# Hybrid attention and convolution layer on one core: prompt attention, output weights and first norm moved to other places of the program

## The reference

```python
s = jnp.einsum('bqhmd,bkhmd->bhmqk', qblk, k).astype(jnp.float32) * scale
p = jax.nn.softmax(s, axis=-1)
a = p[:, :, 0] - lam * p[:, :, 1]
return jnp.einsum('bhqk,bkhe->bqhe', a.astype(v.dtype), v)
...
att = _rms(att, subln_w) * (1.0 - lam_init)
att = att.reshape(b, n, D_ATT) * jax.nn.silu(g_att)
conv = cb * _short_conv(cc * ch, conv_w, conv_b) * jax.nn.silu(g_conv)
y = jnp.concatenate([att, conv], axis=-1) @ w_out
return x + gate * y
```

## Time and profile before

| | us |
|---|---|
| median of 3 runs (lowest, highest) | 1815.07 (1813.13, 1816.41) |
| the profiled execution, own time | 1812.12 |
| its span, first to last instruction | 1810.3 |
| PE matmul busy | 1684.4 (93%) |
| DVE busy | 1044.8 (58%) |
| ACT busy | 789.7 (44%) |
| POOL busy | 753.8 (42%) |

### The profile page before, as it was taken

The page is one execution under the profiler, slowest core; times in us unless marked ns, Lnnn a source line. Parts: engine busy times, 40 slices in busy tenths (PEclk is TensorE's granted clock), DMA queues, the critical chain, the costliest instruction groups (busy, mean ns, idle before and its releaser), DMA issues.

```text
span 1810.3 us, 25375 instructions
## 1 busy us (share of the span) xinstructions
PE 1684.4 (93%) x8526; PEld 1465.4 (81%) x8526; DVE 1044.8 (58%) x1393; ACT 789.7 (44%) x1659; POOL 753.8 (42%) x807
## 2 busy tenths in 40 slices
PE   4899999989999999999589999999999999669999
PEld 1688888879989989999468888888888888558889
DVE  2552887862242322422577777777777777465653
ACT  4562333330010100100288888888888888321110
POOL 0001888860000000000188888888888888200000
PEclk7899999999999999999899999999999999779999
DMA  9962222331020120200541141114011110455441
GB/s 358 292 199 85 105 92 104 105 120 40 31 87 15 41 75 30 73 20 30 141 104 30 35 91 45 33 31 106 29 35 55 56 32 12 148 178 188 166 150 46
DMA packets 131474, 163.69 MB, mean 90 GB/s; under 512 B 10464, under 2 KB 119776, under 8 KB 130272
## 3 DMA queue, kind: packets, MB, share of 16 engines
q1 hardware_dynamic: 126288, 158.61, 27.4%
q10 hardware_dynamic: 5136, 4.46, 0.7%
HBM read 112.95 MB, written 50.07 MB: 90 GB/s over the span
## 4 chain that ended last, share of the span: by engine, by line
PE 76%; DVE 10%; DMA 4%; issue 4%; SPq 2%; ACT 2%; ACTq 1%; POOL 1%; DVEq 0%; POOLq 0%
PE ps L688 38%; PE ps L839 11%; PE ps L914 10%; PE ps L828 9%; PE ps L820 4%; DVE stt L1494 3%; DVE e L1476 2%; PE ps L752 1%; DMA wad<-in_w_ada 1%; PE ps L897 1%; DMA worw<-in_w_out 1%; DVE w L1260 1%; DMA raw<-in_w_in 1%; DVE stt L1518 1%; DMA spill_cv<-scr 1%
## 5 line engine op out<-in xcount | busy, mean ns | idle before, releaser
L688 PE MATMUL ps<-hT,w 128*128 128x448 f32 (+1 forms) x3360 | 688.1, 365 | 12.6 <-DVE w L1260 12.6
L688 PEld LDWEIGHTS ps<-hT,w 128*128 128x128 f32 x3360 | 623.1, 188 | 70.9 <-issue 27.1
L1494 DVE TENSOR_REDUCE stt<-ps 128x1 f32<-128x1024 f32 x256 | 312.6, 1221 | 133.8 <-PE ps L839 131.7
L839 PE MATMUL ps<-kb,qb 128*128 (+1 forms) x1280 | 331.9, 390 | 46.4 <-ACT e L1154 23.6
L1154 ACT ACTIVATE e<-ps,stt 128x1024 f32<-128x1024 f32 x256 | 285.5, 1115 | 139.5 <-DVE stt L1494 139.3
L839 PEld LDWEIGHTS ps<-kb,qb 128*128 128x128 f32 x1280 | 204.3, 191 | 85.5 <-issue 38.2
L828 PE MATMUL ps<-at,vb 128*128 128x256 f32 x1088 | 272.2, 380 | 0.0
L644 POOL TENSOR_TENSOR stt<-stt,lamc 128x2 f32<-128x2 f32 x64 | 12.5, 195 | 579.0 <-DVE stt L1510 579.0
L828 PEld LDWEIGHTS ps<-at,vb 128*128 128x128 f32 x1088 | 203.7, 190 | 35.9 <-issue 0.2
L650 POOL TENSOR_TENSOR e<-e,stt 128x512 f32<-128x512 f32 (+1 forms) x192 | 218.5, 1138 | 5.0
L914 PE MATMUL ps<-mix,wo 128*128 128x448 f32 (+1 forms) x960 | 204.1, 372 | 7.2 <-DVE mix L1564 7.2
(11 more groups left out here) (120 smaller groups left out, 1383.5 us busy)
## 6 DMA issues: line engine op xcount, KB each, us to landing
raw<-in_w_in SPq DMA_DIRECT2D x32, 512.0 KB, 4.0
qb<-spill_q SPq DMA_DIRECT2D x256, 64.0 KB, 2.3
scr<-in_xtok SPq DMA_DIRECT2D x8, 1024.0 KB, 8.0
wad<-in_w_ada SPq DMA_DIRECT2D x4, 2048.0 KB, 17.0
scr<-in_xT SPq DMA_DIRECT2D x8, 1024.0 KB, 6.4
kb<-spill_k SPq DMA_DIRECT2D x8, 1024.0 KB, 9.8
spill_k<-scr SPq DMA_DIRECT2D x32, 224.0 KB, 2.2
spill_q<-scr SPq DMA_DIRECT2D x32, 224.0 KB, 2.2
```

The costliest lines, as they stand in the source:

```text
L688: mm = pe.matmul(out, slot_of(l, j), rhs_of(r, j), start=(i == 0 and j == 0), stop=(i == 2 and j == DJ - 1))
L839: mm = pe.matmul(out[:, c0 - k0:c1 - k0], qb[:, t, ver, m], keys, start=(ver == 0), stop=(ver == 1))
L1494: dve.tensor_reduce(stt[:, b, 0, 3 * m + c:3 * m + c + 1], ps[:, 2 * c:2 * c + 2, :].rearrange("p c n -> p (c n)"), AX.X, ALU.max, negate= ...
```

## The change

Four things change. The tiles in SBUF are laid out anew so that they can be: `at` loses an unused half, the prompt's buffers lie where `wo` comes to lie later, `worw` and `wo` have room of their own beside the loop's tiles, the group's tiles `atr`, `csr`, `gar`, `mixc0`, `mixa0` take over key, query and exponential buffers, `csr` of four slots replaces `csq` and `crs`, and `mix` becomes `mixc` (convolution) and `mixa` (attention).

1. The prompt's attention goes into the loop's first steps: loads ahead of the values' loads, scores on PE after step 0, DVE's six operations in steps 1 and 2, `prompt_exp` after ACT's step 1, transposes after PE's step 2, product after step 3. PE's step 4 waits for `pr_a` 3, as the value products use bank 7 as well.
2. The output weights are loaded in steps 3 to 10 and split at the ends of steps 5 to 12 (`WO0 = 5`), one tile a step.
3. The drain takes in the first group: squares in ACT's step 64, `csums` and roots after it, the four convolution halves after PE's first part of step 65, two heads' `norm` before and two behind DVE's last transposed group. There DVE makes the high part itself (`mine=True`).
4. The first group's loads of convolution and gates go out right behind the loop's last q load.

```diff
             load_q(3, 0, 3 * P)
+            load_prompt()
             load_v(0, 0)
             load_v(0, 1)
 
             sp.wait_ge(stored, 32 + 32 * H * NG)
             sp.wait_ge(aux_stored, 16 * (1 + H + H * NG))
-            load_prompt()
 
             def load_wo(n):
                 wait(sp, c_wlo, n - 1)
                 sp.dma_start(worw[:, n % 2], a["w_out"][n]).then_inc(c_raw[n % 2], 16)
...
             for it in range(ITS):
                 head = it // 4
                 for t in range(4):
-                    sp.wait_ge(s_pair, 4 * (4 * it + t + 1))
-                    if it == 4 * (H - 1) and t == 0:
-                        load_wo(0)
-                        load_wo(1)
+                    n = 4 * it + t
+                    sp.wait_ge(s_pair, 4 * (n + 1))
...
                         load_q(t, (it + 1) // 4, ((it + 1) % 4) * 4 * P + t * P)
...
+                    if WO0 - 2 <= n < WO0 - 2 + DJ:
+                        load_wo(n - WO0 + 2)
+                    if n == NT - 4:
+                        load_att(0)
+
+            load_mix(0)
+            load_gates(0)
             sp.wait_ge(t_mm, 5 * NT)
-            load_gates(0)
-            sp.wait_ge(pv_mm, NT - 2)
-            load_mix(0)
-            load_wo(6)
...
-
+            load_x(0)
             sp.wait_ge(pv_mm, NT)
+            sp.wait_ge(c_wlo, DJ)
             sp.wait_ge(aux_stored, 16 * (1 + H + H * NG + 1))
             for i in range(2):
                 sp.wait_ge(att_stored[i], 16 * ITS)
...
             def prompt_scores():
                 pe.wait_ge(s_p, 16 * (6 * H + 1))
-                pe.wait_ge(exp_done, 4 * NT)
                 for m in range(2 * H):
                     for ver in range(2):
-                        mm = pe.matmul(ps[:, m // 4, (m % 4) * P:(m % 4 + 1) * P], qp[:, ver, m], kp[:, m],
+                        mm = pe.matmul(ps[:, 5 + m // 4, (m % 4) * P:(m % 4 + 1) * P], qp[:, ver, m], kp[:, m],
                                        start=(ver == 0), stop=(ver == 1))
                 mm.then_inc(pr_mm, 1)
...
+                if isinstance(n, int) and n == 0 and g == 0:
+                    pe.wait_ge(pr_v, 2)
...
                     n = 4 * it + t
+                    if n == S_PV:
+                        pe.wait_ge(pr_a, 3)
                     step(it, t, tr=n >= S_TR, tr_last=n > S_TR, pv=n >= S_PV)
+                    if n == 0:
+                        prompt_scores()
+                    if n == 2:
+                        prompt_transposes()
+                    if n == 3:
+                        prompt_product()
             with pe.Fori(2, ITS) as it:
                 for t in range(4):
                     step(it, t)
-            prompt_scores()
-            for n in range(NT, NT + S_PV):
-                step(n // 4, n % 4, sc=False, tr=n < NT + S_TR, tr_last=n <= NT + S_TR)
-                if n == NT + 2:
-                    prompt_transposes()
-                if n == NT + 3:
-                    prompt_product()
...
+                if k < H:
+                    pe.wait_ge(exp_done, 4 * NT)
+                    bank = k
+                else:
+                    bank = 6 + k % 2
+                    if k == H:
+                        pe.wait_ge(t_dve, NT)
+                    elif k == H + 1:
+                        pe.wait_ge(att_evac, NT // 2)
+                    else:
+                        pe.wait_ge(c_std, k - 1)
+                pe.matmul(ps[:, bank, 0:n], ones, csr[:, k % 4, 0:n], start=True, stop=True).then_inc(c_sum, 1)
...
                         pe.wait_ge(c_wlo, o + 1)
                     if o == 0:
                         pe.wait_ge(c_mix[tg % 2], 32 * (tg // 2 + 1))
-                    wait(pe, o_used, k - 3)
+                    if k < H:
+                        pe.wait_ge(c_std, k + 1)
+                    else:
+                        pe.wait_ge(o_used, k - 3)
...
+            step(ITS, 0, sc=False)
             for h in range(H):
                 csums(h, GROUPS[0][1])
-                out_half(0, h, 0)
+            step(ITS, 1, sc=False, tr=False)
+            for o in range(H):
+                out_half(0, o, 0)
+            step(ITS, 1, sc=False, tr_last=False, pv=False)
+            step(ITS, 2, sc=False, tr=False)
+            step(ITS, 3, sc=False, tr=False, tr_last=False)
...
+                    if after and p == 0:
+                        for h in range(H):
+                            square(0, h)
                 if sc:
...
-                    wo_hi(0)
-                    wo_hi(1)
-                    prompt_exp()
-                if n == NT + 2:
-                    act.wait_ge(a_ready, NT)
-                    act.wait_ge(a1_ready, NT)
-                    wo_hi(2)
-                    wo_hi(3)
-                if n == NT + 3:
-                    prompt_hi()
-                    act.wait_ge(t_mm, 5 * (NT - 1))
-                    for o in range(4, DJ):
-                        wo_hi(o)
-            prompt_out()
...
-                wait(act, c_sum, k - 1)
-                act.activation(csq[:, k % 2, 0:n], atr[:, h, 0:n], ACT.Square).then_inc(c_sq, 1)
+                    act.wait_ge(c_at, 16 * (tg + 1))
+                wait(act, c_y1, k - 3)
+                act.activation(csr[:, k % 4, 0:n], atr[:, h, 0:n], ACT.Square).then_inc(c_sq, 1)
 
             def root(tg, h):
                 n = GROUPS[tg][1]
                 k = H * tg + h
                 act.wait_ge(c_sum, k + 1)
-                wait(act, c_y1, k - 1)
-                act.activation(crs[:, k % 2, 0:n], ps[:, 6 + k % 2, 0:n], ACT.Sqrt, scale=1.0 / P, bias=eps[:])\
+                bank = k if tg == 0 else 6 + k % 2
+                act.activation(csr[:, k % 4, 0:n], ps[:, bank, 0:n], ACT.Sqrt, scale=1.0 / P, bias=eps[:])\
                     .then_inc(c_std, 1)
...
+            for it in range(4):
+                for t in range(4):
+                    n = 4 * it + t
+                    step(it, t, tr=n >= S_TR, tr_last=n > S_TR, out=n >= S_OUT and t % 2 == 0, scale=n >= 1)
+                    if n == 1:
+                        prompt_exp()
+                    if n == 3:
+                        prompt_hi()
+                        prompt_out()
+                    if n == 4:
+                        act.wait_ge(aux_stored, 16 * (1 + H + H * NG + 1))
+                    if WO0 <= n < WO0 + DJ:
+                        wo_hi(n - WO0)
+            with act.Fori(4, ITS) as it:
+                for t in range(4):
+                    step(it, t, out=t % 2 == 0)
+            step(ITS, 0, sc=False, after=True)
+            for h in range(H):
+                root(0, h)
+            step(ITS, 1, sc=False, out=False, scale=False)
+            step(ITS, 2, sc=False, tr=False, scale=False)
+            step(ITS + 1, 0, sc=False, tr=False, tr_last=False, scale=False)
...
+            PROMPT_AT = {(1, 0): prompt_max, (1, 1): prompt_shift, (1, 3): prompt_den,
+                         (2, 0): prompt_coef, (2, 1): prompt_scale, (2, 2): prompt_add}
...
+                    if isinstance(n, int) and (n, p) in PROMPT_AT:
+                        PROMPT_AT[n, p]()
...
                 dve.scalar_tensor_tensor(y, atr[:, h, 0:n], sublns[:], rs, ALU.mult, ALU.mult).then_inc(c_y1, 1)
-                if h > 0:
+                if h > 0 and not mine:
                     mix_lo(tg, h - 1)
+                if h == 0:
+                    dve.wait_ge(c_ga, 16 * (tg + 1))
                 dve.wait_ge(c_y1, k + 1)
                 dve.tensor_tensor(y, y, gar[:, h, 0:n], ALU.mult).then_inc(c_y2, 1)
+                if mine:
+                    dve.wait_ge(c_y2, k + 1)
+                    dve.tensor_copy(mixa[tg % 2][:, 0, h, 0:n], y).then_inc(c_hi, 1)
+                    mix_lo(tg, h)
...
+            for it in range(4):
+                for t in range(4):
+                    n = 4 * it + t
+                    step(it, t, den=n >= 1, comb=n >= S_COMB, tr_last=n > S_TR)
+                    if WO0 <= n < WO0 + DJ:
+                        wo_lo(n - WO0)
+            with dve.Fori(4, ITS) as it:
+                for t in range(4):
+                    step(it, t)
+            step(ITS, 0, sc=False)
+            step(ITS, 1, sc=False, den=False, comb=False)
+            dve.wait_ge(a1_ready, NT)
+            dve.wait_ge(t_mm, 5 * (NT - 2))
+            norm(0, 0, mine=True)
+            norm(0, 1, mine=True)
+            step(ITS, 2, sc=False, den=False, comb=False)
+            norm(0, 2, mine=True)
+            norm(0, 3, mine=True)
```

187 lines of the change are left out of this document (80 added, 107 removed).

## The result

The change made the kernel slower: 1838.11 us, the median of 4 runs (1835.23 to 1843.58), against 1815.74 for the kernel before, timed beside it (4 runs, 1813.13 to 1820.05). The ratio is 1.0126, with a 95% interval of 1.0106 to 1.0145. The prediction had the sign right and its range holds the result, but the size not: +11.5 us forecast, +22.4 between the medians, +25.9 between the two profiled spans (1836.2 and 1810.3).

A forecast was written before the change was run, and what follows sets the result against it. PE was taken to bound the loop, busy for 580 of 599 us. The terms +28.5 + 19 - 36 = +11.5 on the profiled 1812.1 gave 1823.6, and 3.0 more for the median 1826.5 us; range 1807 to 1841.

The forecast's parts named there:

- the sign: Whole kernel: the change makes it slower, by +11.5 us on the profiled execution; chance of slower 0.71.
- Part 1: Prompt at the loop's start: PE waits for the last prompt load, then added work in the rounds; +28.5 us, ends 24 and 32.
- nothing covers the wait: Loop's start: step 1 begins 19.7 us later, uncovered because all four engines wait on PE's list.
- Part 2: Weights split in steps 5 to 12: DVE's list becomes the limit; +19 us, ends 0 and 31.
- 12.5 a step against 10.2: Weight steps: 7.9 of DVE work, 0.7 of waits inside, 3.9 at the end; first costs 2.2, seven more 2.4.
- DVE's wait for ACT: Weight steps' end: DVE's subtraction waits for ACT's exponential and factors, 1.6 us, and copy, 1.06 us.
- Part 3: Drain: attention halves begin at 1577.4 instead of 1613.40, on the earlier clock; -36 us, ends 29 and 40.
- the poorer drain: Rival, drain: convolution halves or norms meet a late load, so the gain is only 22 us; 1840.5 us, chance 0.11.
- Free weights: Rival, weight steps: DVE's subtraction slips into its waits, costing 0 instead of 19; 1807.5 us, chance 0.15.
- Contention of DVE and POOL: Rival, weight steps: POOL's work stretches DVE's subtraction by 0.87 us a step, 7 us in all; 1833.5 us, chance 0.12.
- an end of part 1: Loop's start: upper end of 32 us, if the waits hide nothing and the clock stays low for a step.

The follow-up runs named there:

- p_step1: Changed kernel with the prompt's score products one step later, behind step 1's scores, and its DVE operations moved later to match; span 1826.1 us.
- p_load: Changed kernel with the prompt's 25 loads issued ahead of the convolution's last store instead of behind it; span 1828.4 us.
- the companion: Changed kernel with PE's steps 8 to 15 written out instead of run by its loop, nothing else; span 1834.7 us, eight weight steps 107.5 us.
- w_max: Changed kernel with DVE's half of the weight split moved behind the next step's first maximum, ahead of the transposes' copy; span 1819.0 us.
- w_late: Changed kernel with DVE's half of the weight split moved from its step's end to behind the next step's second maximum; span 1814.2 us.
- w_hi_early: Changed kernel with ACT's half of the weight split moved forward, behind its copy of the step's third transposes; DVE's half stays; span 1816.8 us.
- filled3: The companion with second score products done four times in even steps 6 to 12 and twice in odd ones, filling PE's stand; span 1833.3 us.

## Why the prediction was right and wrong

**Part 1, right (+28.5; 30.5 measured).** The time of the products followed from SP's queue and the landing time within 0.2 us, once the loop's later start is taken off (892.72 less 891.04 is 1.68, not 1.64, which changes nothing). The first maximum of step 2 came at 929.93, forecast 929.2 + 1.4. The 2 us beyond the forecast are in the rounds behind it, 1.2 of them in the last, where the product was put in at 0.9 (as four matmuls; the trace has eight, 1.05 us in the drain) and took 2.08 at the low clock behind a stand of 4.4. What the prediction took as given, that nothing covers the wait, was only true of the place: p_step1 and p_load each take a third of part 1 away.

**Part 2, wrong in size (+19; 28.5 measured, 25.7 in the companion).** This is the step that failed: "12.5 a step against 10.2 ... the first costs 2.2 and seven more 2.4". (By its own numbers a step costs 2.3 more, which gives 18.3, and the row at 956.87 has a wait of 1.32 where 1.6 was read; these slips are small.) The mechanism was right, as four kernels show: ACT's half behind its whole step, DVE's behind that, and the next maximum behind it. Two things were left out. The first is the clock: the sum took PE at full clock through all eight steps, as in the earlier trace rows, although the same rows show 0.56 behind a stand; it fell behind the stands of some 2 us, and that is worth 4.3 to 7.1 us. With the clock at 1.00 the waits cost 21.4, only 2.4 more than the 19. The second is that not only the maximum but also `tr_dve` stands behind the subtraction, so that PE meets a second wait inside the step, on its transposes: moving that copy out, once the maximum is out, is worth 5.1 us. Of these 5.1 a part is again clock (0.98 in w_max), so the two terms overlap and don't add to the 19. DVE's wait for ACT, the core of the forecast, was 18.6 us in eight steps, 2.3 a step, where it put 2.7 (1.6 and 1.06).

**Part 3, right (-36; -35.9).** Taken from PE's leaving the loop, every place in it came within about 1 us: the convolution halves, DVE's two heads behind the copy, the wait of 3.25. The term for the poorer drain can be struck; the loads were there. What the prediction did not see is that it forecast its own remedy: DVE stands 3.5 us for the transposes ahead of a copy with two norms behind it, and one of them can go first.

**The rivals.** Free weights: not in this order, but almost in another, 3.3 and 4.5 us for eight splits (85.1 and 86.3 against 81.8). That rival's mechanism, slips into DVE's waits, is true of any place where the subtraction need not wait for ACT. Contention of DVE and POOL: the subtraction took 1.226 us in the change, its uncontended time; moved under POOL's additions it took 1.64 (w_late) and 1.62 (w_hi_early). The Trainium skill (GPSIMD Engine Reference, Key points) says that GpSimd shares its SBUF interfaces with VectorE and contends with instructions of VectorE that have two SBUF inputs; these two rows agree with it, and the change happened to lie outside. The low clock in the loop stood in none of the rivals, only as an end of part 1, and deserved the place.

**The rest of the sum.** The three parts add up to 23.1 of the 25.9 us between the spans. The other 2.8 were in no term: 1.4 of the loop's later start, which is within the scatter of that stage, and 1.4 of the output stage, whose cause stays open. The profiled execution of the changed kernel (1838.14) lay at its median, that of the kernel before (1812.1) 3.6 us below its own, so the medians differ by 3.5 us less than the spans.

## What to carry to other kernels

An operation that waits for another engine's last act of a step costs little where its own engine is idle, and much where it stands ahead of that engine's next urgent work: put it behind the first operations that the bottleneck waits for, and list all of these, not only the first. When such a wait lets TensorE stand, reckon with the low clock for its next microseconds too. And before a change is given up, move its parts one by one: this one cost 22 us as written, and its same parts in other places made the kernel 1.45% faster than before.

## What the hardware showed that was not expected

- The granted clock fell behind a stand of only 1.96 us (with waits of 0.50 and 0.48 us shortly before), in a stretch where PE was otherwise busy. Waits of 0.4 to 1.1 us, which filled3 still has, did not lower it there.
- A stretch of 108.6 us became 4.3 us shorter with 64 more products in it.
- A load of 64 KB costs SP's queue 0.65 us to issue; 24 of them and one of 256 KB are 16 us, and so a queue can bound a start while the DMA engines have room (35% busy from 893 to 909 us of the changed kernel).
